# State-space chunks on VectorE: the next chunk's phases and drive matrices are made before the current chunk's scan instead of after it

## The reference, cut to what matters

```python
def _s5_scan(bu, lam_bar, b_fac, h0):
    b = bu * b_fac
    if h0 is not None:
        b = b.at[:, 0].add(lam_bar * h0)
    a = jnp.broadcast_to(lam_bar, b.shape)
    _, h = lax.associative_scan(_ssm_combine, (a, b), axis=1)
    return h
...
    bu, bu_c = drive(ug), drive(ucg)
    hc_f = _s5_scan(bu_c, *fwd, None)
    hc_b = flip(_s5_scan(flip(bu_c), *bwd, None))
    h_f = _s5_scan(bu, *fwd, hc_f[:, -1])
    h_b = flip(_s5_scan(flip(bu), *bwd, hc_b[:, 0]))
    y = readout(h_f + h_b, ug)
```

## Time and profile before

| | us |
|---|---|
| median of 3 runs | 3243.85 (3241.22 to 3244.2) |
| the profiled execution, its own time | 3243.18 |
| its span in the trace | 3241.4 |
| PE busy | 2913.0 (90%) |
| DVE busy | 2258.4 (70%) |
| ACT busy | 1331.6 (41%) |
| chain that ended last | PE 79%, DVE 12%, ACT 7% |

### The profile page before, as it was taken

One profiled execution on the slowest core, in us unless ns is written; L12 is line 12 of the kernel. 1 busy time (PEld: TensorE's weight loads), 2 busy tenths in 40 slices (PEclk: granted clock), 3 DMA queues, 4 the chain that ended last, 5 costly groups with the idle time before them and its releaser, 6 DMA issues.

```text
span 3241.4 us, 49316 instructions
## 1 busy us (share of the span) xinstructions
PE 2913.0 (90%) x17119; PEld 2405.1 (74%) x17119; DVE 2258.4 (70%) x4422; ACT 1331.6 (41%) x2256; POOL 199.8 (6%) x238
## 2 busy tenths in 40 slices
PE   7999898864799999999999997977881899999998
PEld 5655544543689999999999996766771788888886
DVE  3274441879987777777777775366449998888886
ACT  3122221123964444444444443131311966666663
POOL 0000000000001111111111110000000000000010
PEclk8999999786999999999999999998995999999999
DMA  5522121633257887878777774133241188888885
GB/s 228 192 85 94 49 78 66 271 135 145 97 181 249 291 272 277 288 251 295 254 248 252 255 255 141 62 111 101 95 150 45 55 316 315 316 317 316 316 315 182
DMA packets 164476, 645.09 MB, mean 199 GB/s; under 512 B 15616, under 2 KB 49568, under 8 KB 125216
## 3 DMA queue, kind: packets, MB, share of 16 engines
q1 hardware_dynamic: 135520, 434.15, 38.5%
q0 software_dynamic: 28864, 209.76, 17.7%
HBM read 624.02 MB, written 19.79 MB: 199 GB/s over the span
## 4 chain that ended last, share of the span: by engine, by line
PE 79%; DVE 12%; ACT 7%; issue 1%; DMA 1%; SPq 0%; DVEq 0%; ACTq 0%
PE ps L680 78%; ACT hot L1428 3%; DVE topi L1839 1%; DVE topi L1847 1%; DVE sc L1841 1%; ACT spill L1420 1%; ACT gateA L1417 1%; ACT gateB L1414 1%; DVE top L1836 1%; DVE top L1844 1%; PE ps L788 0%; DVE besti L1847 0%; DVE eq L1883 0%; DVE eq L1879 0%; DVE cand L1841 0%
## 5 line engine op out<-in xcount | busy, mean ns | idle before, releaser
L680 PE MATMUL ps<-h2a,ehi 128*128 128x384 f32 x2048 | 522.0, 335 | 0.0
L1468 ACT ACTIVATE ehi<-ring 128x1024 fp32r<-128x1024 f32 x256 | 271.3, 1060 | 360.9 <-PE ps L680 360.5
L1969 DVE TENSOR_TENSOR elo<-ring,ehi 128x1024 fp32r<-128x1024 f32 x256 | 313.1, 1223 | 106.2 <-ACT ehi L1468 106.1
L680 PEld LDWEIGHTS ps<-h2a,ehi 128*128 128x128 f32 x2048 | 373.1, 188 | 10.3 <-issue 0.5
L680 PE MATMUL ps<-h2b,ehi 128*128 128x192 f32 x2048 | 346.8, 273 | 0.0
L680 PE MATMUL ps<-h2a,elo 128*128 128x384 f32 x1024 | 343.7, 336 | 0.0
L680 PEld LDWEIGHTS ps<-h2b,ehi 128*128 128x128 f32 x2048 | 320.0, 191 | 18.4 <-issue 0.5
L1934 DVE TENSOR_TENSOR elo<-ring,ehi 128x1024 fp32r<-128x1024 f32 x256 | 311.8, 1219 | 12.6 <-ACT ehi L1441 12.6
L680 PE MATMUL ps<-hT,ring 128*128 128x512 f32 (+1 forms) x896 | 308.0, 503 | 0.0
L663 POOL DMA_INDIRECT gbuf<-in_expert_rows,gidx x192 | 183.1, 954 | 1787.6 <-DVE yg L1957 1653.4
L680 PE MATMUL ps<-h2b,elo 128*128 128x192 f32 x1024 | 280.9, 274 | 0.0
(11 more groups left out here) (325 smaller groups left out, 4524.7 us busy)
## 6 DMA issues: line engine op xcount, KB each, us to landing
ring<-in_experts SPq DMA_DIRECT2D x512, 512.0 KB, 5.2
ring<-in_w_mod SPq DMA_DIRECT2D x48, 1024.0 KB, 7.6
ring<-in_w_side SPq DMA_DIRECT2D x24, 1024.0 KB, 4.9
ring<-in_w_front SPq DMA_DIRECT2D x12, 1024.0 KB, 6.4
ring<-in_w_merge SPq DMA_DIRECT2D x16, 768.0 KB, 4.3
ring<-in_w_q SPq DMA_DIRECT2D x12, 1024.0 KB, 5.0
gate_scratch<-spill SPq DMA_DIRECT2D x48, 256.0 KB, 2.0
gateA<-gate_scratch SPq DMA_DIRECT2D x4, 3072.0 KB, 21.3
```

The costliest lines, as they stand in the source:

```text
L680: return pe.matmul(out, w, x, start=start, stop=stop, **k)
L1468: act.activation(ehi[:, 2 + k % 2, :], ring[:, (u + k) % RING, DM:2 * DM], ACT.Copy).then_inc(vhi_ready, 1)
L1969: v.tensor_tensor(elo[:, r, DM:2 * DM], ring[:, r, DM:2 * DM], ehi[:, 2 + b, :].bitcast(F32), ALU.subtract).then_inc(vlo_ready, 1)
```

## The change

VectorE now does `phases(i+1)` and `kernel_in(i+1)` ahead of `states(i)`; `kernel_out(i+1)` and `skip(i+1)` stay behind it. SP issues the load of the next chunk's `s5_bc` ahead of the scratch traffic of the current chunk's taps instead of behind it. No instruction is added or removed, and each function keeps its waits.

```diff
@@ SP @@
                     load(u, a["s5_bc"][l, 0])
                     for k in range(3):
                         load(u + 1 + k, a["w_side"][l, k])
+                    load(u + 4, a["s5_bc"][l, 1])
                     taps(0)
-                    load(u + 4, a["s5_bc"][l, 1])
                     for i in range(1, S5_ITER):
                         load(u + 4 * i + 1, a["w_side"][l, 3 * i])
                         load(u + 4 * i + 2, a["w_side"][l, 3 * i + 1])
-                        taps(i)
                         if i + 1 < S5_ITER:
                             load(u + 4 * i + 4, a["s5_bc"][l, i + 1])
+                        taps(i)
                         load(u + 4 * i + 3, a["w_side"][l, 3 * i + 2])
@@ VectorE @@
                     for i in range(S5_ITER):
-                        states(i)
                         if i + 1 < S5_ITER:
                             phases(i + 1)
                             kernel_in(i + 1)
+                        states(i)
+                        if i + 1 < S5_ITER:
                             kernel_out(i + 1)
                             skip(i + 1)
```

## The result

| | before | changed |
|---|---|---|
| median of 6 runs each, us | 3242.7 (3239.08 to 3246.68) | 3256.85 (3252.68 to 3262.84) |
| the profiled execution, its own time | 3243.18 | 3262.84 |
| its span | 3241.4 | 3261.0 |
| PE busy | 2913.0 | 2926.5 |
| DVE busy | 2258.4 | 2258.9 |

The ratio is 1.0042 (1.0030 to 1.0053): slower by some 14 us, where +4.7 was forecast and the range ended at 3254. The profiled execution of the changed kernel is the slowest of its six runs, so I compare stretches of it, and not its span.

A forecast was written before the change was run, and what follows sets the result against it. TensorE was taken to bound layer 0's stage, a VectorE-TensorE loop layer 1's. Layer 0 +11.2, layer 1 +4.7 and -11.2 net +4.7 us: 3247.9 against the profiled execution, 3248.5 as median, range 3242 to 3254.

The forecast's parts named there:

- What bounds the kernel: Layer 0's stage is 99.5% TensorE; in layer 1 VectorE and TensorE wait for each other in a loop.
- Part 2, the gaps in chunk 0: Both layers: moved work delays `states(0)`, so TensorE idles before `read(0)`, 9.75 us in layer 0 and 9.7 in layer 1.
- The clock behind the gaps: Half clock after TensorE's idle time before both `read(0)` costs 1.45 us each, bounds 0 to 3.0.
- The upper bound of 3.0: Most that half clock could cost behind each gap before `read(0)`, in us: double the 1.45 taken.
- Part 1, the gain in layer 1: Steps from chunk 1 to 2 and 2 to 3: `taps` to `taps` 38.8 us instead of 44.4, -11.2 together.
- the 6.5 of 11.2 - 4.7: Layer 1: two later steps gain 11.2 us together, less `taps(1)` coming 4.7 us late after chunk 0.
- the +4.7: Whole kernel: net forecast loss in us, from +11.2 in layer 0, +4.7 and -11.2 in layer 1.
- its rival: Layer 1, chunks 1 and 2: late `s5_bc` load holds up `states`, costing 8.8 us, net +13.5, 3257.3 us; chance 0.27.
- The clock rival: Layer 1: clock holds before the three `taps`, giving back 4.4 us, net +0.3, 3244.2 us; chance 0.10.
- the rival without a stall: Chunk 0 of both layers: `read(0)` not late, layer 0 unchanged, net -17.7 us, 3226.2 us; chance 0.05.
- the upper bound of 10.8: Largest net loss in us: 4.7, plus 3.1 for double clock cost, plus 3.0 for both loads late.

The follow-up runs named there:

- l0_only: Changed kernel with the new VectorE order in layer 0 alone, the old one in layer 1, loads as changed; 3255.34 us, ratio 1.0033.
- from_chunk1: Changed kernel, but chunk 0 of both layers keeps the old VectorE order; load of `s5_bc` stays ahead of the scratch traffic; 3236.57 us, ratio 0.9971.
- the second trace: The changed kernel run once more, nothing altered, to get another trace of it; 3258.59 us, ratio 1.0038 to the kernel before.
- filled11: Changed kernel with 11 additional matmuls, result unused, on TensorE ahead of `read(0)` of each layer; 3250.49 us, ratio 1.0015 to the kernel before.
- order_only: Changed kernel with SP's load of `s5_bc` put back behind the scratch traffic, new VectorE order kept in both layers; 3286.28 us, ratio 1.0122.
- shift8: Kernel before the change with 8 additional matmuls, result unused, on TensorE at the very end of layer 1's stage; 3253.98 us, ratio 1.0028.
- shift6: Kernel before the change with 6 additional matmuls, result unused, on TensorE at the very end of layer 1's stage; 3247.52 us, ratio 1.0010.

## Why the prediction was wrong, by its own steps

- **What bounds the kernel**: right. Layer 0 is TensorE's, and gained nothing in any run; layer 1 is the loop of both engines.
- **Part 2, the gaps in chunk 0**: right in place, cause and size. 9.75 and 9.7 us were named, and 9.80 and 9.72 measured, released by `hx`, with `phases(1)` released by `tables(0)`. l0_only and from_chunk1 show that this is the loss.
- **The clock behind the gaps**: the mechanism right, the term too small. 1.45 us each was taken from `taps`, but `read` lost 2.4 us in each layer (5.1 instead of 2.7), and in the second trace too; filled11 got back 2.6 us in layer 0. The upper bound of 3.0 held for `read`. The error is that I took the price of one piece of work for a gap as the price of the gap: the clock stayed at 0.50 through the whole of `read`, and `read` is the longer piece. In the same way I left `taps` of layer 1 at 3.45 and what stands behind them at its old time. In the changed kernel's trace the way from `taps(1)` to `drive(1)` took 0.9 us more and that from `taps(3)` to `drive(3)` 0.8 (1.84 and 1.65 us for `weights` instead of 1.1).
- **Part 1, the gain in layer 1**: 38.8 us from `taps` to `taps` were named and 39.8 and 39.1 measured (39.3 and 39.0 in the second trace), so the gain is 4.6 to 5.4 us a step and not 5.6. Of the 1.0 us missing in the first step, 0.9 is the clock behind `taps(1)`, and next to nothing the load, though `kernel_in` waited 0.76 us for it; the 0.3 missing in the second is `read(2)`, late by the states. With `taps(1)` late by 5.5 to 6.0 us instead of 4.7, mostly since `read(0)` was slower than I had taken, layer 1 as a whole gave 3.2 to 4.4 us and not the 6.5 of 11.2 - 4.7. `taps` stayed at half clock, as taken, though TensorE's idle time fell to 4.2 us.
- **The step that failed is one that the sum made in silence**: that all work outside the stage costs what it did. It cost 4.1 us more, at the two places where the granted clock was 0.82 and 0.84 in place of 1.00. With the mis-sized terms inside the stage, +1.2 for layer 0 and +3.3 for layer 1, most of it the clock's, it makes the +4.7 into 13.3. I read the clock only beside the changed gaps and never asked what a shift of the stage's end does to the clock's course in the 960 us behind it. What decides whether these 4 us come stays open.
- **The rivals**: "slower" came true, but not by its rival. Late states made `read` late by 0.4 us in all in chunks 1 and 2 of layer 1 (0.7 in the second trace), not by the 8.8 it would have needed, and order_only shows what it would have looked like: 47.1 us of waits for the load and 29 us more. The clock rival and the rival without a stall were wrong as the rows said they would be.
- The range was too narrow because both its ends were built from bounds inside the stage alone. There they held: 12.4 - 3.2 = 9.2 us lies under the upper bound of 10.8.

## What to carry to other kernels

Work moved ahead in a loop is free only if every turn has the idle time for it, the first one above all: here two steps of layer 1 could win, layer 0 could win nothing, and chunk 0, whose `drive` follows `taps` at once, lost more than all the rest won. The size to move is that of the idle time, not of a whole function group: `phases` (3.7 us) fits where `phases` and `kernel_in` (10.8 us) don't, and the version that also filled the other engine's gap with work that it has to do anyway (`side(2)`) won 28 us, where the best of the others, VectorE's new order from chunk 1 on with the moved loads (from_chunk1), won 7. No run separates the parts of that version. And a forecast of a few us in a kernel whose TensorE clock rises and falls needs a margin of some 4 us for work that isn't touched.

## What the runs showed of the hardware that was not expected

- The same matmuls behind the stage took from 960.2 to 965.1 us in the thirteen traces, in kernels that don't differ there. The 4 us between the kernel before and the changed one are at two places, where the granted clock was 0.82 and 0.84 instead of 1.00. The start of that work, counted from the start of the span, doesn't tell which it is (2292.46 and 2292.19 us gave 960.8 and 964.9).
- Two more matmuls ahead of that work (1.7 us, shift8 against shift6) made 6.5 us in the medians.
- Adding 19 us of useless matmuls (filled11) to the changed kernel made it 8 us faster. 4 to 5 of these are seen in the two stages, the greater part as `read(0)` back at 2.6 us instead of 5.1 in each.
- A matmul of 512 fp32 columns appears as two records, and took 0.87 us (17.33 us for 20).
